# When a product into four PSUM banks waits for each bank, and how its first 48 matmuls are ordered

## The reference, cut to what matters

```
merged = gates[:, :, 0] * y_sb + gates[:, :, 1] * y_swa
x = x + merged @ w_out[l]                                  # "out", 1024 x 1024
x = x + jnp.square(jax.nn.relu(h2 @ w_up[l])) @ w_down[l]  # "down", 4096 x 1024
...
def _swiglu(x, w1, w3, w2):
    return (jax.nn.silu(x @ w1) * (x @ w3)) @ w2           # "f1d" and "f2d", 2816 x 1024
...
return merged @ w_o                                        # "wo", 1024 x 1024
return o @ wo                                              # "xo", 512 x 1024
```

## Time and profile before

| what | value |
|---|---|
| median of 3 runs | 2433.6 us (2433.56 to 2435.38) |
| the profiled execution's own time | 2436.49 us |
| its span | 2434.4 us |
| PE busy | 2320.4 us, 95% of the span |
| DVE, ACT, POOL busy | 57%, 46%, 8% |
| granted TensorE clock, mean | 0.989 of full speed |

### The profile page before, as it was taken

One profiled execution on the slowest core, in us unless ns is written; L12 is line 12 of the kernel. 1 busy time (PEld: TensorE's weight loads), 2 busy tenths in 40 slices (PEclk: granted clock), 3 DMA queues, 4 the chain that ended last, 5 costly groups with the idle time before them and its releaser, 6 DMA issues.

```text
span 2434.4 us, 38470 instructions
## 1 busy us (share of the span) xinstructions
PE 2320.4 (95%) x16084; PEld 2126.8 (87%) x16098; DVE 1388.0 (57%) x1838; ACT 1119.4 (46%) x1737; POOL 186.5 (8%) x191
## 2 busy tenths in 40 slices
PE   7988999998999999999998999999999999998998
PEld 6987987887898998798998889879978999887997
DVE  5556555545654544655566664555465555776454
ACT  4753543573453444445443544444434445344442
POOL 0001110001120210000002001111100000110110
PEclk9999999999999999999999999999999999999999
DMA  6423554532555655554533545556555544263554
GB/s 212 136 96 129 187 196 165 181 122 96 171 182 193 211 185 187 162 181 141 174 106 119 175 156 182 182 184 198 182 161 189 160 156 140 79 199 128 189 178 138
DMA packets 109005, 395.93 MB, mean 163 GB/s; under 512 B 12374, under 2 KB 12544, under 8 KB 108576
## 3 DMA queue, kind: packets, MB, share of 16 engines
q1 hardware_dynamic: 104400, 377.53, 47.1%
q0 software_dynamic: 4432, 15.93, 2.0%
HBM read 392.92 MB, written 1.05 MB: 162 GB/s over the span
## 4 chain that ended last, share of the span: by engine, by line
PE 85%; DVE 8%; ACT 3%; issue 2%; DMA 1%; POOL 0%; SPq 0%; DVEq 0%; ACTq 0%; POOLq 0%
PE psum L388 76%; DVE w_low L345 2%; PE psum L790 2%; PE psum L756 2%; PE psum L692 2%; ACT w_high L342 1%; DMA ring<-in_weights 1%; PE psum L774 1%; ACT attn_p L872 1%; DVE stats L562 1%; PE psum L1746 1%; DVE mx L816 1%; DVE xs L2058 0%; DVE xs L585 0%; DVE xT_low L651 0%
## 5 line engine op out<-in xcount | busy, mean ns | idle before, releaser
L345 DVE TENSOR_TENSOR w_low<-ring,w_high 128x1024 fp32r<-128x1024 f32 x704 | 863.9, 1255 | 606.9 <-ACT w_high L342 605.8
L342 ACT ACTIVATE w_high<-ring 128x1024 fp32r<-128x1024 f32 x704 | 717.9, 1052 | 316.0 <-DMA ring<-in_weights 315.7
L388 PE MATMUL psum<-xT_high,w_high 128*128 128x256 f32 x2976 | 847.5, 285 | 0.0
L388 PE MATMUL psum<-xT_low,w_high 128*128 128x256 f32 x2976 | 842.8, 283 | 0.0
L388 PE MATMUL psum<-xT_high,w_low 128*128 128x256 f32 x2976 | 842.8, 283 | 0.0
L388 PEld LDWEIGHTS psum<-xT_high,w_high 128*128 128x128 f32 x2976 | 572.2, 192 | 0.8
L388 PEld LDWEIGHTS psum<-xT_low,w_high 128*128 128x128 f32 x2976 | 572.1, 192 | 0.4
L388 PEld LDWEIGHTS psum<-xT_high,w_low 128*128 128x128 f32 x2976 | 571.8, 192 | 0.0
L388 PE MATMUL psum<-w_high,hidden 128*128 128x512 f32 x1216 | 378.2, 391 | 7.0 <-DVE attn_pT L2048 5.0
L388 PEld LDWEIGHTS psum<-w_high,hidden 128*128 128x128 f32 x1216 | 228.8, 188 | 55.3 <-issue 8.1
L388 PE MATMUL psum<-w_low,hidden 128*128 128x512 f32 x608 | 237.0, 390 | 0.0
(11 more groups left out here) (233 smaller groups left out, 2201.3 us busy)
## 6 DMA issues: line engine op xcount, KB each, us to landing
ring<-in_weights SPq DMA_DIRECT2D x706, 512.0 KB, 3.5
pages<-in_affine POOLq DMA_DIRECT2D x16, 512.0 KB, 5.1
ring<-in_weights SPq DMA_DIRECT2D x8, 440.0 KB, 3.3
pages<-in_gains POOLq DMA_DIRECT2D x4, 512.0 KB, 4.4
pages<-in_mem POOLq DMA_DIRECT2D x2, 1024.0 KB, 7.3
ring<-in_weights SPq DMA_DIRECT2D x4, 384.0 KB, 3.2
x<-in_x_in SPq DMA_DIRECT2D x2, 512.0 KB, 4.3
pages<-in_rows POOLq DMA_DIRECT2D x2, 512.0 KB, 6.0
```

The costliest lines, as they stand in the source:

```text
L342: eng.activation(high, raw, ACT.Copy).then_inc(self.flag("w_rounded").sem, 1)
L345: eng.tensor_tensor(self.w_low[:, piece % SLOTS, 0:width], raw, high.bitcast(F32), ALU.subtract).then_inc(self.flag("w_split").sem, 1)
L388: m = pe.matmul(out, a, b, start=(first and i == 0), stop=(last and i == len(pairs) - 1))
```

## The change

`take_bank` moves from ahead of the whole product to the first product of each group (`k == 0`), so that only the bank of (0,0) is waited for at the start. The first two steps (`HEAD = 2`) are ordered by bank: both steps of (0,0), both of (0,1), both of (1,0), both of (1,1). From the third step on, the order is the former one. With four steps, `xo` has `last = 0` and so `head = 0`: its order stays, and only its waits move.

```diff
+HEAD = 2
...
-        for t in range(NT):
-            for n in range(2):
-                self.take_bank(pe, l, banks, (key, t, n))
...
-        order = [(k, t, n) for k in range(last) for t, n in groups]
+        head = min(HEAD, last)
+        order = [(k, t, n) for t, n in groups for k in range(head)]
+        order += [(k, t, n) for k in range(head, last) for t, n in groups]
         order += [(k, 0, n) for n in range(2) for k in tail] + [(k, 1, n) for k in tail for n in range(2)]
         for i, (k, t, n) in enumerate(order):
             if turn is not None and i == len(order) - 2:
                 turn(0)
+            if k == 0:
+                self.take_bank(pe, l, banks, (key, t, n))
             w = self.weight(pe, l, stream, (key, 0, k))
```

## The result

| | before | changed |
|---|---|---|
| median | 2434.65 us (5 executions, 2433.56 to 2435.39) | 2420.58 us (5 executions, 2415.40 to 2426.57) |
| ratio | | 0.994, 95% interval 0.9929 to 0.995 |
| profiled execution, time and span | 2436.49, 2434.4 us | 2415.40, 2413.3 us |

The kernel became faster by 14 us, where 19.6 had been forecast, and its median lies 0.6 us above the range given. The profile, however, is that of the fastest of its five executions, and its span is 21.1 us shorter, close to the 19.0 + 1.6 = 20.6 of the sum. So two questions are left: whether each term of the sum is there, and what the other executions have in them.

What follows compares the result with a forecast made beforehand. PE was taken to bound the kernel (85% of the chain), idling at ten product starts. From the 2433.6 us median, 19.0 for the waits and 0.6 for the clock gave 2414.0 us, range 2411 to 2420.

Steps and rivals of the forecast that it cites:

- The wait at the start: At ten model product starts, PE no longer waits for banks: 16.6 us idle plus small terms, 19.0 us gained.
- both small terms: Per start, 0.16 us from beginning before the modelled end and 0.08 us from no slow matmul after a standstill.
- I carry the whole 19.0: Behind the products, the gain at the starts was taken to reach the kernel's end in full, 19.0 us.
- The first piece is given back later: Released after seven products instead of four; eighth piece tight at `wo`, bound 0.3 us each, cost taken as 0.
- Nothing arrives sooner: At `wo`, the eighth piece was assumed split no earlier than before, bounding PE's wait from above at 0.3 us.
- The clock: A fall to 1.2 GHz at `out`, layer 0, would go: 1.6 us in the profile, 0.6 us in the median.
- The base: Whole kernel before the change: median 2433.6 us, from which the forecast gain of 19.6 us was taken.
- A: Rival for the whole kernel: full gain as summed, 2412 to 2417 us; chance 0.78.
- B: Rival at `out` and `wo`: late eighth piece (1.7 us per `wo`) or queues return gain, mostly 2417 to 2421; chance 0.15.
- C: Rival at every start: another wait takes the bank's place, so no gain, 2433 us; chance 0.04.
- D: Rival at the starts: second weight piece split late, losing 2.0 us per start, 2454 us; chance 0.03.
- its threshold: Second piece split later than 0.68 us after the old start makes that start slower than before.

Runs made afterwards that it cites:

- first-bank order: Changed kernel, but only (0,0) takes its first two steps together; two runs, 12 executions, median 2413.6 us, ratios 0.9924 and 0.9925 to the kernel before.

## Why the prediction was wrong

*The wait at the start, 19.0 us.* Right, in mechanism, place and size: all ten waits are gone, both small terms are seen, the ten starts give 18.9 us in the trace, and the order alone gives nothing.

*"I carry the whole 19.0".* The step that failed. At equal clock the whole kernel gained 15.5 us (span times clock, 48 executions before against 16 changed, uncertainty 0.6); the plain means differ by 15.3. So 3.4 us of what the starts give are not there at the end. Of these, 1.2 to 1.9 were put at nothing in the next term. The other 1.5 to 2.2 stay open: the three traces of the changed kernel together (2389.8 us at equal clock, against 2407.5 and 2406.6 in the two traces that have all ten waits) do not show them, and what was lost there is no more than the waits at `wo`.

*The first piece is given back later, "I take 0".* Wrong; the bound of 0.3 us at each `wo` that stood beside it was the better value, and even it was passed. The slot does come free 0.6 us earlier: the eighth piece is issued 4.98 us after the start of `wo`, layer 0, instead of 5.59 after where it would have started. But its transfer took 6.05 us instead of 5.23, so that it landed 0.2 us later than before; in layer 1 it took 6.11 instead of 5.47. "Nothing arrives sooner" was thus no bound from above. What made it longer: the next piece is now issued 0.67 us behind it instead of 2.72, and it is itself issued 1.1 us behind POOL's load instead of 1.7. With POOL's load away and the next piece as near as that (0.68 us) it took 3.70, so the load is needed for the loss; how much of the added 0.8 us is the next piece's is not shown. Measured: 0.32 to 0.90 us of idle time per `wo`, and with 0.24 us each for stopping and starting again 1.2 to 1.9 us in all. A tenth of the gain. Two runs that mend it in different ways take the waits away, so this cause is shown.

*The clock, "I take off ... 0.6 for the clock".* Not confirmed: over all executions the mean granted clock is the same before and after, 0.9883 and 0.9881, which is known to about 1 us of time, so that 0.6 can't be told from nothing. The removed idle time did take its own falls away, 4 in 12 starts against none in 40; others appeared elsewhere.

*The range.* Far too narrow. I let the clock fall once more or less, 1.6 us each way, while the executions of the changed kernel lie between 2415.4 and 2427.5 and those of the first-bank order between 2412.2 and 2429.0, mostly by the clock. The rule of the Trainium skill (TensorE: Matmul & The Clock Gate, Part 1), that the gate's schedule does not restart with a kernel and slow matmuls vary from run to run, had been cited against the 1.6 us, and the runs agree with it (mean clocks of 0.985 to 0.990 in one program); I did not draw from it that the range had to be wider. Whether the median of five fell inside 2411 to 2420 was then a matter of luck: it missed by 0.6 us, the median of all 16 executions, 2419.6, lies inside by 0.4. The centre, 2414.0, was off by 5.6 us all the same.

*The base.* The median of three, 2433.6, was itself a lucky one: 48 executions have 2435.5. The five first ones within 2 us of each other led me to trust it to a microsecond. Of the 5.6 us, 1.9 are the base, 0.6 the clock, and the rest, some 3, the part of the 19.0 that did not arrive.

*The rivals.* What came is between A and B: B's mechanism at `wo` is real and its price was 1.5 us instead of 3.4. C did not occur. D is real at four steps and absent at two, as its threshold says: `w_split` of the second piece was never waited for.

## What to carry to other kernels

Take each buffer when it is reached, not all at the start: the wait that this hides can be the last reader's whole queue (2.4 us at `out` and `wo`), not just its read-out, and here the move of the waits gave nearly everything while the reordering gave about as much as it took. A reordering that uses a piece longer gives its slot back later; ask which transfer is then tight, and with what it shares the bus. When a gain is below 1%, forecast the median of executions, not the profiled one: find the spread that the clock makes among executions of the same kernel first, and let the range hold it.

## What the runs showed of the hardware

Executions of one program on one core differ by up to 17 us of 2413 (2412.15 to 2428.95), with a mean clock of 0.991 to 0.983; over 12 executions the time follows the clock with a correlation of -0.99. Standing still for 2.4 us was followed by 1.2 GHz at 4 of 12 starts, and at the same instruction in one trace and not in another. Without the stop, 0 of 40 starts were. Removing these stops still left the mean clock of all executions where it was (0.9883 and 0.9881).

Of four transfers of 512 KB that were issued within 1.8 us (two of POOL's load, the eighth piece, the next one), the eighth piece took 6.05 us from issue to landing, where 3.12 were seen at `out`. With POOL's two moved ten us away it took 3.70.
